# A square root's argument rewritten, and two weight splits moved ahead of the LRU gates

## The reference

```
def rg_lru_branch(xr, xg, conv_w, conv_b, wa, ba, wx, bx, lam):
    xr = causal_depthwise_conv(xr, conv_w, conv_b)
    ...
    log_a = LRU_C * jax.nn.sigmoid(gate_r) * jax.nn.log_sigmoid(lam)
    a = jnp.exp(log_a)
    u = jnp.sqrt(-jnp.expm1(2.0 * log_a)) * (jax.nn.sigmoid(gate_i) * xr)
    _, h = lax.associative_scan(_linear_combine, (a, u), axis=1)
    return (h * jax.nn.gelu(xg)).astype(xr.dtype)
```

## Time and profile before

| what | us |
|---|---|
| median of 3 runs (lowest, highest) | 2109.34 (2109.34, 2110.01) |
| the profiled execution, its own time | 2110.01 |
| span from its first to its last instruction | 2108.2 |
| PE busy / weight load busy | 1922.9 / 1754.9 |
| DVE busy | 1423.6 |
| ACT busy | 1168.3 |

### The profile page before, as it was taken

How to read it: one execution, slowest core, us unless ns; L and a number is a source line. 1 busy time by engine, 2 the same in 40 slices (tenths; PEclk the granted TensorE clock), 3 DMA queues, 4 the chain that set the end, 5 groups by cost and what they waited for, 6 DMA issues and landing times.

```text
span 2108.2 us, 30304 instructions
## 1 busy us (share of the span) xinstructions
PE 1922.9 (91%) x12946; PEld 1754.9 (83%) x12946; DVE 1423.6 (68%) x1424; ACT 1168.3 (55%) x1310; POOL 76.5 (4%) x94
## 2 busy tenths in 40 slices
PE   4999997988999999997997999898769999999997
PEld 3989997987998889997997999797658888888885
DVE  3686547536555677637644555757569999999995
ACT  2553344545444554333644444455368888888884
POOL 0000013000000000013000000000000000000000
PEclk9999998998999999998998999899779999999998
DMA  7334364534554433356542555333249999999993
GB/s 270 121 140 142 121 258 160 200 106 146 190 196 144 155 141 130 126 177 245 184 159 93 199 190 182 139 121 120 104 177 366 375 375 377 381 377 376 375 388 139
DMA packets 64524, 440.87 MB, mean 209 GB/s; under 512 B 7372, under 2 KB 7372, under 8 KB 14592
## 3 DMA queue, kind: packets, MB, share of 16 engines
q1 hardware_dynamic: 55296, 399.63, 50.4%
q0 software_dynamic: 8096, 35.30, 4.5%
q10 hardware_dynamic: 992, 3.93, 0.5%
HBM read 428.61 MB, written 10.23 MB: 208 GB/s over the span
## 4 chain that ended last, share of the span: by engine, by line
PE 66%; DVE 22%; ACT 8%; issue 2%; POOL 1%; DMA 1%; DVEq 0%; ACTq 0%; POOLq 0%
PE psum L188 64%; DVE ring_low L202 6%; ACT hl L198 3%; DVE arena L212 3%; DVE ht L202 2%; DVE rounded L202 2%; DVE rounded L212 2%; DVE arena L202 2%; ACT arena L198 2%; PE psum L192 1%; POOL arena L202 1%; DVE hl L202 1%; ACT gn L198 1%; ACT rounded L198 1%; ACT L198 1%
## 5 line engine op out<-in xcount | busy, mean ns | idle before, releaser
L202 DVE TENSOR_TENSOR hl<-ring,hl 128x2048 fp32r<-128x2048 f32 (+1 forms) x190 | 433.8, 2286 | 336.7 <-ACT hl L198 336.3
L188 PE MATMUL psum<-ht,hl 128*128 128x256 f32 x4992 | 630.0, 288 | 15.9 <-DVE hl L202 10.3
L188 PEld LDWEIGHTS psum<-ht,hl 128*128 128x128 f32 x4992 | 616.5, 195 | 25.1 <-DVE hl L202 10.9
L198 ACT ACTIVATE hl<-ring 128x2048 fp32r<-128x2048 f32 (+1 forms) x286 | 536.2, 1896 | 138.5 <-PE psum L188 125.4
L188 PE MATMUL psum<-hl,ax 128*128 128x512 f32 (+1 forms) x1608 | 352.7, 356 | 5.9 <-DVE ax L202 4.8
L198 ACT ACTIVATE arena<-psum 128x512 f32<-128x512 f32 (+5 forms) x232 | 121.0, 522 | 422.3 <-PE psum L188 409.3
L188 PEld LDWEIGHTS psum<-hl,ax 128*128 128x128 f32 x1608 | 265.8, 192 | 46.9 <-DVE ax L202 5.5
L202 DVE TENSOR_TENSOR ring_low<-ring,hl 128x2048 fp32r<-128x2048 f32 x96 | 215.4, 2286 | 23.0 <-ACT hl L198 22.9
L188 PE MATMUL psum<-arena 128*128 128x128 f32 (+6 forms) x1520 | 194.5, 297 | 21.4 <-ACT arena L198 12.4
L188 PEld LDWEIGHTS psum<-arena 128*128 128x128 f32 (+2 forms) x1520 | 178.6, 183 | 32.9 <-ACT arena L198 13.6
L188 PE MATMUL psum<-hl,ht 128*128 128x256 f32 (+1 forms) x1056 | 132.7, 288 | 26.8 <-DVE ht L212 24.0
(11 more groups left out here) (121 smaller groups left out, 1896.4 us busy)
## 6 DMA issues: line engine op xcount, KB each, us to landing
ring<-W SPq DMA_DIRECT2D x284, 1024.0 KB, 5.1
arena<-W SPq DMA_DIRECT2D x48, 1024.0 KB, 7.6
ht_raw<-W SPq DMA_DIRECT2D x46, 1024.0 KB, 7.6
gate_d<-arena POOLq DMA_DIRECT2D x32, 256.0 KB, 3.8
arena<-gate_d POOLq DMA_DIRECT2D x8, 1024.0 KB, 8.0
gn<-GB POOLq DMA_DIRECT2D x10, 512.0 KB, 4.0
arena<-GB POOLq DMA_DIRECT2D x6, 512.0 KB, 5.0
ring<-W SPq DMA_DIRECT2D x4, 512.0 KB, 4.8
```

Of the source, the lines that this page charges most:

```text
L188: return Nothing() if self.e is None else self.e.matmul(o, a, b, start=start, stop=stop, skip_group_check=skip_group_check)
L198: return self.e.activation(o, a, f, bias=bias, scale=scale)
L202: return Nothing() if self.e is None else self.e.tensor_tensor(o, a, b, op)
```

## The change

Two edits. First, the two splits of `w_out`'s first half move, on both engines: on ACT from behind the GELU's tanh to ahead of the tanh of `wa` and `wx`; on DVE from behind `log_weight(3)` to ahead of the small instructions on lam, log a and `log_weight(2)`. Second, the argument of the square root is computed from t3 = tanh(log a) alone: before, as −(a² + 1)·t3 with the sign put in by the activation's scale; now as 2·t3/(t3 − 1), with a reciprocal. Three DVE instructions stand where two stood.

```
@@ scalar @@
             copy(b2.xg, half(banks["xg",]), "xg")
             gone("xg")
+            for _ in range(4):
+                unit()
             for nm, dst, o in (("wa", t1, 0), ("wx", t2, 2)):
                 ac.wait_ge(s_pe, P[nm])
...
             ac.wait_ge(s_dve, V["uvar"])
-            act(t1, t1, ACT.Sqrt, "ustd", scale=-1.0)
+            act(t1, t1, ACT.Sqrt, "ustd")
             ac.wait_ge(s_dve, V["gelu"])
             act(t3, t3, ACT.Tanh, "gelu", scale=math.sqrt(2.0 / math.pi))
-            for _ in range(4):
-                unit()
             weights(3)
@@ vector @@
             log_keep(2)
             unit()
+            for _ in range(4):
+                unit()
             ve.wait_ge(s_act, A["lam"])
...
             ve.wait_ge(s_act, A["t3"])
-            tt(t1, aL, aL, MUL)
-            stt(t1, t1, 1.0, t3, ADD, MUL, "uvar")
+            ts(t1, t3, -1.0, None, ADD, None)
+            rec(t1, t1)
+            stt(t1, t3, 2.0, t1, MUL, MUL, "uvar")
             tt(t3, b2.xg, b2.xg, MUL)
...
             log_weight(3)
-            for _ in range(4):
-                unit()
             ve.wait_ge(s_act, A["ya", 2])
```

## The result

| | before | after |
|---|---|---|
| median, us (lowest, highest; 8 runs each) | 2108.89 (2104.5, 2110.01) | 2122.48 (2115.85, 2128.05) |
| the profiled execution: time / span, us | 2110.01 / 2108.2 | 2118.27 / 2116.5 |
| D: from taps(1)'s start to bout's start, us | 51.23 | 63.63 |

The kernel is slower by 13.6 us at these medians, where 13.7 was forecast. The ratio is 1.006 (95% interval 1.0048 to 1.0074); it is taken over all 29 executions of the changed kernel, whose median is 2121.49, so by it the loss is 12.6 us (10.1 to 15.6). The profiled execution grew by only 8.3 us. That splits into 3.8 us less ahead of taps(1) (1433.25 before, 1429.44 after, the same code in both), 12.4 more in the stretch D, and 0.3 less behind bout.

A forecast was written before the change was run, and what follows sets the result against it. It took the kernel as one long serial chain with PE busy 66% of the span. Restart +12.2, clock +2.85, no longer late at cmean −1.3 gave +13.7 on 2109.34: 2123.0 us, range 2119.5 to 2127.0 (about 8 in 10).

The forecast's parts named there:

- B's landing: Weights of w_out's second moved split: DMA issued when taps(1) ends at 1440.46, landing 4.9 us later at 1445.36.
- The bank turn: PSUM banks needed up to taps(1) are freed before the splits: no deadlock, PE stops inside scores(3), z(3,1) needing wa's bank.
- Restart of PE: After the stall PE starts weighted(2) at 1454.05 instead of about 1441.87, a shift of 12.18 us.
- The clock: After restarting at weighted(2), PE runs 5.7 us at 1.2 GHz before returning to 2.4 GHz, losing 2.85 us.
- The reciprocal hidden by 0.7 us: Ahead of sums(3): uvar 3.1 us dearer on DVE, yet log_keep(3) ends at 1464.12, PE ready 0.7 us later at 1464.79.
- the rival that had the reciprocal fully on the path: Clock high or PE restarting sooner, so log_keep(3) sets sums(3); 13 to 15.5 us in all; chance 15%.
- What is given back: DVE, without its two splits in front, is no longer late at the cmean subtraction: −1.3 us, subtraction shifted by 13.72.
- Behind cmean: cvar, group norms and cpw keep their length, bout starts 13.7 later; clock fall there worth up to 1.3 either way.
- The bounds of the parts: Landing ±0.3 us; no clock fall 13.1; first 7.1 us slow 14.4; later stretch up to 1.3 either way; together 11.7 to 16.
- The wait does not bite: Rival: second split's weights there below about 1438, both splits fit DVE's and ACT's idle gaps; −0.5 us, 2108.8; 3%.
- Only a short wait: Rival: second split's load depends on taps(0) alone, PE restarts about 2 us late, no clock fall; 1.3 to 4 us; 5%.
- The clock stays low through taps(3): Rival: PE slow through taps(2), sums(3) and taps(3); cmean shifted up to 26.6 us, total 2131 to 2136; chance 7%.

The follow-up runs named there:

- A alone in the gap: Kernel before, only w_out's first split moved, behind t3's tanh on ACT and t2's product on DVE, old formula; 2109.72 us (1.0008), again 2106.32 (0.9993).
- B loaded early: Changed kernel, but the second moved split's weights loaded into memory free after projection xg, without waiting for taps(1)'s slot; 2111.22 us, ratio 1.002.
- 17 + 8 idle matmuls: Changed kernel plus idle matmuls of constants, 17 ahead of z(3,0) and 8 ahead of weighted(2), overwritten by real ones; 2123.22 us, ratio 1.0075.
- B back at its place: Changed kernel with only the first split at the new place on both engines, the second at its old one; 2107.80 us, ratio 1.0001.

## Why the prediction was right

*B's landing* was the key number: expected t0 + 12.11, measured 12.02 (issue at 7.21, 4.81 to land). *The bank turn*: taps(1) ran as before and PE stopped inside scores(3), after z(3,0), as worked out. *Restart of PE*: weighted(2) expected at t0 + 20.80, measured 20.82; both queues behind the splits carry it, in the shares 8.5 (ACT) and 3.7 (DVE) that the run with ACT's move alone shows.

The Trainium skill's page DMA: Bandwidth & Descriptors, section Bandwidth, has 6.15 us for 1 MB issued by GpSimd. The 4.8 us measured here for SP's queue disagree, and the measurement decides. By the page's figure the loss would have been 1.25 us larger than forecast, an estimate.

*The clock* was mis-sized, in the right direction: 5.7 us at 1.2 GHz were expected after the restart, 3.9 came (about the same in the changed kernel's second profile). weighted(2) and taps(2) took 10.07 us from the first's start to the second's end against 8.06 before, so 2.0 us were lost, not 2.85. The two rows that I took the 5.7 from were two cases of something that varies more: `cpw`, started at 1470.22 at the low level in the kernel with A alone in the gap, was at 2.4 GHz again after 2.8 us, bout in the kernel with the formula alone after 6.1, and the router's 7.0 us before never.

*The reciprocal hidden by 0.7 us* failed, through that same term. With PE ready at t0 + 30.9 instead of 31.5, log_keep(3) (expected 30.87, measured 31.0) came last by 0.17 us, so the chain passes the reciprocal. Its share of the loss is small all the same: D differs by 0.4 between the kernels with and without it. In the totals this can't be seen: the move alone came out 11.0 us over before, the changed kernel 13.6 and 13.0, with intervals that overlap. Of the rival that had the reciprocal fully on the path, only this much came true: which engine is last.

*What is given back*: the cmean subtraction was expected 13.72 us later and came 13.33 later; the two splits no longer stand ahead of it, and DVE waits 3.03 us there.

*Behind cmean* I held the length the same. It shrank by 0.9 us. 0.8 of that is gn(2), which took 1.13 us instead of 2.08, with the clock at 1.00 in this execution. cvar with gn(0), the place that I had named, took 2.87 us instead of 4.55, but DVE was busy all through it and only 0.1 reached bout. So the size was inside the 1.3 I allowed, and the place was wrong. So the stretch grew by 12.4 in the profile against 13.7 forecast. That the medians' 13.6 agrees with the forecast to 0.1 us is luck: over all 29 executions it is 12.6, the terms above were off by up to 0.9 us, and the profiled executions of all kernels here begin taps(1) anywhere from 1429.4 to 1435.8 with the same code ahead of it. The bounds of the parts, too, add up to 11.5 at the low end (13.1 − 1.3 − 0.3), not to the 11.7 written.

*The wait does not bite*, the rival of the other sign, is refuted by ACT's 10.46 us. Its mechanism is shown to exist, though, where the landing allows it: the run with A alone in the gap gains the 1.3 us in the stretch. *Only a short wait* is refuted by B's issue at t0 + 7.21; the kernel with B loaded early is that case made real. PE restarted 2.3 us late there and the total was up by 3.6, inside the rival's 1.3 to 4, but the clock did fall, which the rival had excluded. *The clock stays low through taps(3)* did not happen.

The Trainium skill's page TensorE: Matmul & The Clock Gate, section HAM oscillation, says that a PE which waits for a transfer between bursts is throttled again and starts the next burst slow. The trace agrees: the granted clock went from 1.00 to 0.50 near 1440.5, and the 3.9 us behind the restart ran at 1.2 GHz. Here PE didn't read the transfer itself; the wait reached it through two other engines' queues.

## What to carry to other kernels

Before filling an engine's idle gap with work from later, find when that work's input arrives, and what that arrival waits for: here the gap was real, but the transfer was tied to the very matmuls after it. Work with a late input, put early in an in-order queue, costs everything behind it, on every engine that shares the turn of buffers; divide it, and move only the part whose input is there. Count the extra idle time of PE twice, once as time and once as the slower clock that may follow, and check what else becomes last when either goes.

## What the runs showed of the hardware

Short idle times of PE can bring the granted clock down: 2.07 us ahead of sums(3) (17 + 8 idle matmuls) and 2.40 us ahead of weighted(2) (B loaded early) were followed by a fall to 1.2 GHz within 0.5 us of resumed work. 1.89 us ahead of sums(3), in the kernel with B back at its place, was not, though a shorter idle time was, ahead of cvar in the kernel before (the granted clock is 0.97 in 1462.50:1463.00 and 0.50 from there):

```profile
1462.83 4.55 PE L188 MATMUL psum<-arena,cst 128*128 128x256 f32 x12 [1.75 <-DVE arena L202]
```

So the length of the idle time alone didn't decide it. Matmuls that nobody reads kept PE at 2.4 GHz from the end of taps(1) to weighted(2), 13.6 us, and cost nothing where they ended before the wait did: weighted(2) started at t0 + 20.75, 20.82 without them. With 17 + 8 of them the fall came at the next idle stretch; with four more there it stayed away up to 1480, and the time was still no better. A RECIPROCAL of 128x512 took 3.35 us, five times the 0.69 of a SCALAR_TENSOR_TENSOR of that shape. Two 1 MB transfers on SP's queue, issued within 0.4 us of each other, landed after 4.7 and 6.8 us; one alone took 4.8.
